# Recurrent and latent stages in one block, w_out begun with its own splits, group means as two rounded products

## The reference, cut to what matters

```python
def group_layer_norm(x, g, b, n_groups):          # first block, convolution branch, 8 groups of 128
    mu = jnp.mean(xf, axis=-1, keepdims=True)
    var = jnp.mean(jnp.square(xf - mu), axis=-1, keepdims=True)
    y = ((xf - mu) * lax.rsqrt(var + EPS)).reshape(shp)
...
    o = rms_norm(o, onorm_g.reshape(HG_HEADS, HG_HEAD_DIM))   # first block, each head of 128
...
    y = jnp.concatenate([y_conv, y_hgrn.astype(y_conv.dtype)], axis=-1)
    h = h + y @ w_out[i].astype(y.dtype)
    pe = p[i] @ w_pp[i].astype(p.dtype)
    gate = jax.nn.sigmoid(rms_norm(h, pe_norm_g[i]) @ w_pg[i].astype(h.dtype))
    h = h + gate * pe.astype(h.dtype)
...
        u = rms_norm_2(h, norm_mix_g[l])                      # second block
        proj = u @ w_in[l]
        x_rnn, g_rnn, q_c, kv_c, k_pe, gate_logits = jnp.split(proj, split_points, axis=-1)
        xa = causal_conv(x_rnn, conv_w[l], conv_b[l])
        ya = rg_lru(xa, ...) * jax.nn.gelu(g_rnn)             # recurrent stage
        yb = mla(q_c, kv_c, k_pe, positions, ...)             # latent stage, attention
```

## Time and profile before

| | |
|---|---|
| median of 3 runs | 2914.78 us (2914.42 to 2917.72) |
| profiled execution, own time | 2912.4 us |
| its span | 2910.4 us |
| mean granted TensorE clock | 0.971 of full speed |
| PE busy | 2719.5 us (93%) |
| DVE busy | 1652.7 us (57%) |
| ACT busy | 1234.8 us (42%) |
| loop over heads, first start of `scores(i, 0)` to the last | 136.8 to 752.9 us |
| w_out's first product | 934.98 us |
| first latent product | 1676.16 us |

### The profile page before, as it was taken

One profiled execution on the slowest core, in us unless ns is written; L12 is line 12 of the kernel. 1 busy time (PEld: TensorE's weight loads), 2 busy tenths in 40 slices (PEclk: granted clock), 3 DMA queues, 4 the chain that ended last, 5 costly groups with the idle time before them and its releaser, 6 DMA issues. The chain is left out here.

```text
span 2910.4 us, 33765 instructions
## 1 busy us (share of the span) xinstructions
PE 2719.5 (93%) x12640; PEld 2148.8 (74%) x12640; DVE 1652.7 (57%) x2524; ACT 1234.8 (42%) x1733; POOL 206.3 (7%) x183
## 2 busy tenths in 40 slices
PE   7999999999998999999999998999999989599993
PEld 5888888888876887768777697777767668477772
DVE  5788888888532314434324233666767663666664
ACT  4244443434421214634433424555555542266661
POOL 0010111110100000000000000000000000442213
PEclk9999999999999999999999998999999999699997
DMA  5333232332335120112112020000000131899997
GB/s 183 109 120 123 87 102 94 105 105 98 127 119 188 48 102 22 44 58 70 46 50 65 29 80 21 24 15 24 15 24 16 58 75 45 342 358 341 356 363 269
DMA packets 168688, 329.06 MB, mean 113 GB/s; under 512 B 17831, under 2 KB 125480, under 8 KB 154840
## 3 DMA queue, kind: packets, MB, share of 16 engines
q1 hardware_dynamic: 152952, 289.25, 28.5%
q0 software_dynamic: 14720, 34.64, 3.2%
q10 hardware_dynamic: 864, 3.15, 0.3%
HBM read 293.94 MB, written 100.16 MB: 135 GB/s over the span
## 5 line engine op out<-in xcount | busy, mean ns | idle before, releaser
L398 PE MATMUL PS<-UHI,WHI 128*128 128x512 f32 x1008 | 416.0, 413 | 4.1 <-DVE ULO L127 4.1
L398 PE MATMUL PS<-ULO,WHI 128*128 128x512 f32 x1008 | 400.3, 397 | 0.0
L398 PE MATMUL PS<-UHI,WLO 128*128 128x512 f32 x1008 | 400.2, 397 | 0.0
L127 DVE TENSOR_TENSOR WLO<-arena,WHI 128x1024 fp32r<-128x1024 f32 x94 | 115.3, 1226 | 213.9 <-ACT WHI L123 213.8
L398 PEld LDWEIGHTS PS<-UHI,WHI 128*128 128x128 f32 x1008 | 190.6, 189 | 52.3 <-issue 5.5
L398 PEld LDWEIGHTS PS<-ULO,WHI 128*128 128x128 f32 x1008 | 190.7, 189 | 47.6 <-issue 5.5
L398 PEld LDWEIGHTS PS<-UHI,WLO 128*128 128x128 f32 x1008 | 190.3, 189 | 46.4
L1238 PE MATMUL PS<-U2HI,WHI 128*128 128x512 f32 x480 | 193.0, 402 | 2.7 <-DVE WLO L127 2.7
L1238 PE MATMUL PS<-U2HI,WLO 128*128 128x512 f32 x480 | 189.5, 395 | 0.0
L1238 PE MATMUL PS<-U2LO,WHI 128*128 128x512 f32 x480 | 189.4, 395 | 0.0
L1888 PE MATMUL PS<-arena 96*128 96x512 f32 (+3 forms) x384 | 155.1, 515 | 12.5 <-ACTq L2030 10.3
(11 more groups left out here) (458 smaller groups left out, 5895.8 us busy)
## 6 DMA issues: line engine op xcount, KB each, us to landing
arena<-in_w_in SPq DMA_DIRECT2D x88, 512.0 KB, 4.0
xd_dram<-in_x SPq DMA_DIRECT2D x32, 768.0 KB, 6.8
y_dram<-in_x SPq DMA_DIRECT2D x32, 768.0 KB, 6.7
arena<-in_w_gate SPq DMA_DIRECT2D x13, 1024.0 KB, 7.2
arena<-in_w_up SPq DMA_DIRECT2D x13, 1024.0 KB, 11.4
arena<-in_w_down SPq DMA_DIRECT2D x13, 1024.0 KB, 14.0
arena<-in_w_out SPq DMA_DIRECT2D x32, 256.0 KB, 2.6
RB<-in_w_gate SPq DMA_DIRECT2D x7, 1024.0 KB, 7.3
```

Of the source, the lines that this page charges most:

```text
L127: return eng.tensor_tensor(dst, src, hi.bitcast(F32), ALU.subtract)
L398: last = pe.matmul(o[:, h * HALF:(h + 1) * HALF], x[:, k, :], y[:, k, h * HALF:(h + 1) * HALF], start=(k == r == 0), stop=(k == ND - 1 and ...
```

## The change

**Means.** The mean matrix is rounded once into `MEANR` (1/128 is exact). For each mean ACT now rounds the operand into `AVGHI` and DVE computes the remainder into `SQLO` or `HSQLO`; PE does two rounded products per half (high and remainder) instead of one in plain float32. New on ACT: `conv_hi(i)` behind `head_root(i - 1)`, and a rounding behind the square in `conv_square` and `head_square`. New on DVE: `conv_lo(i)` in front of `update(i, 1)`, `square_lo(i)` behind `masked(i, 3)`, `head_square_lo(i)` in front of the last two taps.

**Order in the loop.** On PE `conv_var` goes from behind `scores(i, 3)` to behind `scores(i, 4)`. On ACT `conv_root` goes from behind `mix(i, 4)` to behind `mix(i, 5)`, and `conv_out` from behind `mix(i, 5)` to behind `mix(i, 6)`. On DVE `norm` goes from behind `update(i, 4)` to behind `update(i, 5)`. Scores 5 and 7 use other banks, with waits to match.

**Blocks.** A `retire` (which keeps five semaphores) now stands between the first block and w_out. The latent block is merged into the block of w_out and the recurrent stage, with no barrier and no `retire` between. SP loads the first four latent chunks before it stores the last gate; ACT and DVE split the first two before the last evacuation of the recurrent stage; the rotary tables move from chunk 1 to chunk 3.

**w_out.** ACT and DVE begin with the splits of chunk 0; the feature copies come behind them (PE waits for these only ahead of its fifth output tile), and the recurrence constants go to chunk 18.

```diff
-        SCORES = [LOW] + [PS[:, b, :] for b in (6, 4, 5, 4, 6, 5, 6)]
+        SCORES = [LOW] + [PS[:, b, :] for b in (6, 4, 5, 4, 5, 4, 5)]
...
-                def mean_of(o, v, done):
+                def mean_of(o, hi, lo, done):
                     for h in range(2):
-                        last = pe.matmul(o[:, h * HALF:(h + 1) * HALF], mean, v[:, h * HALF:(h + 1) * HALF],
-                                         start=True, stop=True)
+                        for r, v in enumerate((hi, lo)):
+                            last = pe.matmul(o[:, h * HALF:(h + 1) * HALF], MEANR[:], v[:, h * HALF:(h + 1) * HALF],
+                                             start=(r == 0), stop=(r == 1))
...
-                    if q in (2, 3, 4):
-                        pe.wait_ge(s_amask, (LEVELS + 1) * i + (1, 1, 3)[q - 2])
-                    elif q == 5:
-                        pe.wait_ge(s_croot, i + 1)
-                    elif q >= 6:
-                        pe.wait_ge(s_amask, (LEVELS + 1) * i + (4, 6)[q - 6])
+                    if q >= 2:
+                        pe.wait_ge(s_amask, (LEVELS + 1) * i + max(1, q - 1))
...
                 def turn_keys(i):
                     pe.wait_ge(s_upd, LEVELS * (i + 1))
-                    pe.wait_ge(s_amask, (LEVELS + 1) * i + 7)
+                    pe.wait_ge(s_amask, (LEVELS + 1) * (i + 1))
...
                 def state_steps(i):
                     pe.wait_ge(s_kdec, i + 1)
-                    pe.wait_ge(s_amask, (LEVELS + 1) * (i + 1))
+                    pe.wait_ge(s_croot, i + 1)
...
                     scores(i, 3)
-                    conv_var(i)
                     first_half(n + 2)
                     scores(i, 4)
+                    conv_var(i)
                     second_half(n + 2)
...
+                def conv_hi(c):
+                    act.wait_ge(s_conv, c + 1)
+                    if c:
+                        act.wait_ge(s_oms, c)
+                    split_hi(act, AVGHI[:], ACC[c % 2]).then_inc(s_acchi, 1)
...
                     if i:
                         head_root(i - 1)
+                    conv_hi(i)
                     upper(n + 2)
...
                     mix(i, 4)
-                    conv_root(i)
                     upper(n + 4)
                     mix(i, 5)
-                    conv_out(i)
+                    conv_root(i)
                     evacuate(n + 2)
                     upper(n + 5)
                     mix(i, 6)
+                    conv_out(i)
...
                     taps(c, 3, 5)
+                    conv_lo(i)
                     update(i, 1)
...
                     masked(i, 3)
+                    square_lo(i)
                     taps(c, 8, 11)
                     lower(n + 4)
                     update(i, 4)
-                    norm(i)
                     masked(i, 4)
                     taps(c, 11, 14)
                     lower(n + 5)
                     update(i, 5)
+                    norm(i)
                     masked(i, 5)
...
-                    taps(c, 20, 24)
+                    taps(c, 20, 23)
                     lower(n + 7)
                     state(i)
-                    taps(c, 24, 27)
-                    taps(c, 27, CONV_K)
+                    taps(c, 23, 29)
+                    head_square_lo(i)
+                    taps(c, 29, CONV_K)
...
+        retire(s_held, s_x3, s_ptok, s_wpp, s_yland)
...
-        retire(s_held)
...
+                store_gate(NB - 1, 0)
+                sp.wait_ge(s_mt, 2 * NB)
                 for n in range(NRAW):
-                    load(n)
+                    load_latents(n)
+                store_gate(NB - 1, 1)
+                for t in range(2):
+                    sp.wait_ge(s_sigst[t], 16 * NB)
...
+                    for n in range(4, NX):
+                        if n == NX - 1 and not more:
+                            for k in range(2):
+                                stream_hi(act, k, W6RAW, W6HI, s_w6land, s_w6used, s_w6hi)
+                        evacuate(b, n, more)
...
-                act.wait_ge(s_pturn, 1)
-                act.activation(PFEAT[:, 1, :], banks(6), ACT.Copy).then_inc(s_pfeat, 1)
                 upper(0)
...
                 for n in range(4 * ND):
                     stream_hi(act, n, W3RAW, W3HI, s_w3land, s_w3used, s_w3hi)
+                    if n == 0:
+                        act.wait_ge(s_pturn, 1)
+                        act.activation(PFEAT[:, 1, :], banks(6), ACT.Copy).then_inc(s_pfeat, 1)
+                    if n == 18:
+                        act.wait_ge(s_soft, 1)
+                        act.activation(CREC[1], CREC[1], ACT.Exp, scale=-1.0).then_inc(s_softexp, 1)
```

More of the change, by code:

```diff
@@ new lines, in _ @@
+                sp.wait_ge(s_u2n, NT)
+                for n in range(2, NX):
+                    sp.wait_ge(s_rwlo, n - 1)
+                    load(0, n)
+                    if n == 2:
+                        load_gates(0)
+                with sp.Fori(1, NB) as b:
+                    for n in range(NX):
+                        sp.wait_ge(s_rwlo, NX * b + n - 1)
+                        hold(sp)
+                        load(b, n)
+                        if 1 <= n <= 2:
+                            store_gate(b - 1, n - 1)
+                        if n == 2:
+                            sp.wait_ge(s_ri, 2 * b)
+                            hold(sp)
+                            load_gates(b)
@@ L1816, in _, with project @@
             def _(pe):
+                def project(b, n, halves=(0, 1)):
+                    if halves[0] == 0:
+                        pe.wait_ge(s_rwlo, NX * b + n + 1)
+                        if n >= 2 or not isinstance(b, int):
+                            pe.wait_ge(s_revac, NX * b + n - 1)
+                    o, w = banks(2 * (n % 2)), weight_of(b, n)
+                    for h in halves:
+                        for k in range(ND):
+                            for i, (x, y) in enumerate(passes((w[1][n % 2], w[2][n % 2]), (U2HI, U2LO))):
+                                last = pe.matmul(o[:, h * HALF:(h + 1) * HALF], x[:, k, :],
+                                                 y[:, k, h * HALF:(h + 1) * HALF],
+                                                 start=(k == i == 0), stop=(k == ND - 1 and i == 2))
+                    if h:
+                        last.then_inc(s_rproj, 1)
@@ new lines, in lru_gates @@
+                def lru_gates(b, t):
+                    pe.wait_ge(s_ax, 32 * b + 32)
+                    pe.wait_ge(s_xa, 2 * b + 2)
+                    if t or not isinstance(b, int):
+                        pe.wait_ge(s_riev, 2 * b + t)
+                    for i in range(2):
+                        for h in range(2):
+                            for k in range(2):
+                                last = pe.matmul(banks(4 + 2 * i)[:, h * HALF:(h + 1) * HALF],
+                                                 WAX[:, i, k, t * P:(t + 1) * P],
+                                                 XA[k][:, h * HALF:(h + 1) * HALF], start=(k == 0), stop=(k == 1))
+                    last.then_inc(s_ri, 1)
@@ new lines, in embed @@
+                def embed(m):
+                    if m:
+                        pe.wait_ge(s_gated, m)
+                    else:
+                        pe.wait_ge(s_wpp, 32)
+                        pe.wait_ge(s_h, NT + 6)
+                    for h in range(2):
+                        for k in range(2):
+                            last = pe.matmul(PS[:, 4 + h, :], PFEAT[:, k, m * P:(m + 1) * P],
+                                             WPP[:, k, h * HALF:(h + 1) * HALF], start=(k == 0), stop=(k == 1))
+                    last.then_inc(s_peprod, 1)
@@ new lines, in gate @@
+                def gate(m, k0, k1):
+                    if k0 == 0:
+                        pe.wait_ge(s_nlo, m + 1)
+                        if m < 2:
+                            pe.wait_ge(s_h, NT + 4 + 4 * m)
+                        else:
+                            pe.wait_ge(s_gsig, m - 1)
+                    for k in range(k0, k1):
+                        if m == 0:
+                            pe.wait_ge(s_pglo, k + 1)
+                        for h in range(2):
+                            for i, (x, y) in enumerate(passes((NHI, NLO), (WPGHI, WPGLO))):
+                                last = pe.matmul(PS[:, gate_banks(m) + h, :], x[:, k, m * P:(m + 1) * P],
+                                                 y[:, k, h * HALF:(h + 1) * HALF],
+                                                 start=(k == i == 0), stop=(k == ND - 1 and i == 2))
+                    if k1 == ND:
+                        last.then_inc(s_gprod, 1)
@@ new lines, in _ @@
+                turn_h(0)
+                embed(0)
+                for m in range(NT):
+                    gate(m, 0, 4)
+                    if m:
+                        embed(m)
+                    if m + 1 < NT:
+                        turn_h(m + 1)
+                    gate(m, 4, ND)
```

(11 more changed lines are left out.)

881 lines of the change are left out of this document (406 added, 475 removed).

## The result

The changed kernel takes 2922.4 us (median of 7 runs, 2919.24 to 2929.05) against 2915.56 (7 runs, 2914.42 to 2917.72) before, a ratio of 1.0026 with a 95% interval of 1.0014 to 1.0037. The forecast was 2916.3. The range holds the time; the difference, 6.8 us, lies just above the 0.2% (5.8 us) that the prediction called no change, with the interval on both sides of it. The profiled execution has a span of 2920.3, 9.9 more than before.

| stretch | forecast | measured |
|---|---|---|
| up to the first scores 0 | 0 | +1.1 |
| head 0 | +1.2 | +3.1 |
| heads 1 to 6 | +18.6 | +17.9 |
| head 7 to the last product of the block | -1.5 | +0.3 |
| seam to w_out, and w_out | -6.5 | -4.6 |

A forecast was written before the change was run, and what follows sets the result against it. PE, busy 93% of the span, bounds the kernel, with DVE close behind in the loop. First block +18.3, w_out -6.5, latents -10.3 sum to +1.5: 2913.9 profiled, 2916.3 median. Range 2888 to 2929 us.

The forecast's parts named there:

- The mean: On PE in the loop: a mean costs 0.94 us, 0.77 less than before, for each of 24 means.
- Step 1: Start of a head: conv_hi (1.0 us) and conv_lo (1.2) lie exposed, so DVE's first update starts 6.6 behind scores 0.
- Step 2: PE waits 0.6 us for masked copy 0 before scores 2, and 0.4 for masked copy 1 before the mean.
- step 5: Late in a head: masked copy 7 ends at 56.1 us; PE waits 2.2 before scores 7 and the keys' turn.
- Step 4: Root behind mix 5 delays the weight split and fifth update; PE loses 2.2 us before scores 6.
- Head 7: Last head of the first block: no taps, so no waits, and -1.5 us.
- The seam to w_out: First block to w_out: products start 4.6 us earlier and 1.9 of lost clock returns; -6.5, at the least -4.1.
- The latents: Seam to latents: PE goes straight on, then waits 3.2 us before chunk 4; -10.3 (-13.5 without wait, -8 if clock falls).
- PE never waits in the loop: Rival: DVE's work fits and PE has no loop waits; 2879.5 us, chance 0.12.
- only the root's hole: Rival: only the wait between mix 5 and mix 6 stays, 2.2 us less 2.3 a head; 2895, chance 0.16.
- The clock falls in the new holes: Rival: clock falls in the hole before scores 6, heads 0 to 6, 1.9 us each, 13 together; 2929, chance 0.12.
- The merged block gives nothing back: Rival: at the latents, early loads or splits come no sooner; 2926 us, chance 0.08.

The follow-up runs named there:

- three edits: Changed kernel with the root in front of mix 5, two taps moved forward and the convolution's rounding behind the weight split: 2896.3 us, ratio 0.9935, head 87.6 us.
- four: Changed kernel with root before mix 5, two taps forward, convolution rounding behind the weight split, and scores 7 in bank 6: 2888.3 us, ratio 0.9912, head 86.7 us.
- the taps forward: Changed kernel with two of DVE's convolution taps moved from behind the state recurrence into its wait for a weight split: 2920.0 us, ratio 1.0015.
- the new blocks alone: Changed kernel with the loop of the kernel before; only the merged block, new retire and early w_out stay: 2899.3 us, ratio 0.9949.
- the new means alone: Kernel before with the means of two rounded products and the new loop order, blocks and seams as before: 2936.8 us, ratio 1.0075.
- without remainders: Changed kernel without the means' three remainders on DVE, each mean adding the rounded data twice: 2908.3 us, ratio 0.9980.
- root: Changed kernel with ACT taking the convolution's inverse root before mix 5, not behind it: 2902.3 us, ratio 0.9962.
- later rounding: Changed kernel with ACT rounding the convolution behind the weight split, not in front of it: 2924.0 us, ratio 1.0031.

## Why the prediction was right, and where not

**The mean.** Right: 0.92 for 0.94.

**Step 1, the chain from the head's mean.** Right that `conv_hi` and `conv_lo` come exposed before update 1, wrong in what follows. I had update 1 at 6.6 behind scores 0; it is at 4.66, because scores 0 itself starts later, behind the hole before `pad`'s reader. **Step 2's** waits before scores 2 (0.6) and the mean (0.4) are absent for the same reason.

**The step that failed** is the sentence behind step 5: "`state`, the taps and `head_square_lo` (1.2) have room", resting on DVE's wait of 3.62 in the earlier trace rows. That wait lies behind `pad`; before it there is little room. The rows of before that I had not costed (DVE, and the head's mean on PE):

```profile
372.86 1.23 DVE L127 TENSOR_TENSOR WLO<-arena,WHI 128x1024 fp32r<-128x1024 f32 x1 [2.10 <-ACT WHI L123]
...
387.25 0.69 DVE L820 TENSOR_TENSOR arena<-PS,arena 128x512 f32<-128x512 f32 x1
```

```profile
387.89 1.88 PE L443 MATMUL PS<-RC,square 128*128 128x512 f32 x4
```

`pad`'s first half was there at 387.94, and PE, with a mean of 1.71 from 387.89, wanted it at 389.60: 1.66 of slack. From the split's remainder to the end of that half are 15.08 before and 17.61 after (382.19 to 399.80), 2.53 more: the new remainder and one more tap. The mean is 0.77 shorter. 1.66-2.53-0.77 = -1.64, the hole of 1.63.

**Step 4, the root.** The mechanism was right: DVE's wait of 2.6 measured 2.44, and its removal gave 2.5 a head. PE shows only 1.13 before scores 6, since the hole before `pad`'s reader has made it late already. With 0.16 for each hole, PE has lost 1.8+1.3 = 3.1 up to scores 6; the walk had 1.0+2.2 = 3.2.

**Step 5, scores 7 and the keys' turn.** 2.2 forecast, 0.78+1.05 measured, 2.15 with 0.16 for each; the bank alone is worth 0.95 of it (three edits against four).

**The loss a head** was forecast as 5.4 over PE's own 85.8, and 91.1-85.8 = 5.3 measured. The walked chain closes on itself (head mean, head root, splits, DVE's list, update 5, masked copy 7, the keys' turn, the next head mean), and its length was right: with the taps forward, where 1.06 of `pad`'s hole is gone, a head still takes 91.1. Which stretch of PE pays for it is another matter, and there I was wrong. That the way over `pad`, which I had not costed, came out equal and not longer is luck: both reach update 2 within 0.1 us. Head 0 has the full +3.1 because what I let it save lies in front of its scores 2, and the holes (1.11, 0.78, 1.05, 1.63 there too) lie behind; head 6 has only +1.7, since no `pad` follows it.

**Head 7** has no taps, as said. That a hole of 3.68 stands before the products of the last splits, where it was 2.89, is the last mean, 0.77 shorter, which the forecast had rightly not counted as a gain. But I had "no waits", and scores 6 met a hole of 0.67, behind the root. The rest of the way from -1.5 to +0.3 is clock, about 1 us behind that hole before the last splits' products, in the changed kernel and in the kernel before (windows of PE; 24 products against 28 in 8 us):

```profile
853.31:861.31 8.00, 8.00 (x24) 0.66 0.48 162
```

```profile
831.88:839.88 8.00, 8.00 (x28) 0.79 0.51 159
```

**The seam to w_out.** First product 4.3 earlier for 4.6: `retire` cost 2.73-1.65 = 1.08 for my 1.0, and from the barrier's end to the first product 4.3 passed for my 4.2. The term that failed is the 1.9 of clock, which I had the shorter hole give back; here only 0.3 came of it. With the new blocks alone it did come: 6.6 less for my 6.5. The Trainium skill, "TensorE: Matmul & The Clock Gate", section "What's actually happening", has activity as what releases the clock; the 4.6 that the prediction worked out by that rule is what this profile shows, and not that of the new blocks alone, where a like hole cost no clock.

**The latents.** The mechanism was right, wait and all (3.2 forecast, 2.62 measured): from the gate store to chunk 4's load pass 7.15 us (1688.39 to 1695.54), where I had 8.0. -9.1 for -10.3. With the new blocks alone the clock did not fall there, and the stretch took 10.9 less; here it fell behind the hole before chunk 4 (window of PE), the case for which I had given -8:

```profile
1705.75:1707.75 2.00, 2.00 (x7) 0.50 0.48 130
```

**The recurrent stage** holds a difference that no step had, and no edit made (one window before, one after):

```profile
1261.50:1267.50 6.00, 5.94 (x25) 4.81 (x26) 0.03 (x3) 0.02 (x1) 0.00 (x0) 1.00 0.51 164
```

```profile
1279.30:1285.30 6.00, 5.97 (x14) 4.72 (x15) 0.00 (x0) 0.00 (x0) 0.00 (x0) 0.50 0.53 170
```

These are the same products before and after, behind the same hole of 2.37 us. At half the clock they cost 2.9 us more. The kernel with the new means alone, that with the new blocks alone and that without remainders kept the full clock there; the seven other variants did not, and lost 1.3 to 2.9.

**The time as a whole.** Between the forecast's +1.5 and the +9.9 of the profiled execution lie 8.4 us. About 6 are clock (1.9 at w_out, 2.9 in the recurrent stage, 1.2 at the latents), 3.7 are heads 0 and 7, of which 1 is clock again; the rest takes 1.2 back.

**The rivals.** "PE never waits in the loop" and "only the root's hole" fell with the rows above. "The clock falls in the new holes" did not come true inside the loop of the changed kernel (1.00 from 130 to 780 us, with holes of up to 1.98), and held at the seams, where it was not placed. It was a near thing: two variants lost 1.5 us behind such a hole of the loop once and twice, at `pad`'s reader and not before scores 6. "The merged block gives nothing back" fell: -15.8.

## What to carry to other kernels

A saving on the busiest engine can be worth nothing in a loop whose other engines must deliver on a serial path: here 2.3 us of PE a head came with 5.3 of waits, and four changes of order, with no work removed, turned +21.7 us into about -11 (2888.3 against the 2899.3 of the blocks alone). To find the path, look not at the engine that shows the hole but at what the engines upstream wait for (ACT idle for 7.08 us beside the root that everybody waited for), and read slack at each consumer of its own: a wait further down the same list is no room for what comes before it. When removing a hole gives nothing, look for a second way of the same length to the same consumer, and try both edits together. And look at the granted clock stretch by stretch before a few us are put down to an edit: it fell in places that the edit had not touched.

## What the runs showed of the hardware

Whether TensorE's clock falls behind a hole of 2 to 3.7 us is not settled by its length. Behind the 2.37 us of the recurrent stage the granted clock fell to 0.50 in 8 of 12 profiles (the two kernels and the ten variants) and stayed at 1.00 in 4. In the loop, in heads 3 and 4 of four kernels (changed, means alone, root, later rounding), the hole before `pad`'s reader was 1.97 to 2.01: it fell behind three of these eight. Behind the loop's holes of up to 1.78 it never fell. At w_out, in the ten with the merged block, it fell in 7. In four of them it fell just behind the second hole (2.40 to 2.56 us), and in three it had fallen among the transposes, behind the first (2.73 or 2.74); these then took longer, which left a second hole of only 1.49 to 1.67. It stayed full in 3, with second holes of 2.28, 2.43 and 2.45 behind first ones of 2.71 to 2.74. Behind the 3.68 us at the end of the first block it stayed full in two variants (root, later rounding). At w_out, in the loop and in the recurrent stage a fall cost 1.3 to 2.9 us, as much as several terms of the forecast; what decides it stays open.

Of six taps of DVE beside POOL's products (386.24 to 395.13) four took 1.28 us each, as the taps without POOL do. The second, beside the end of POOL's longest product (2.13 us from 386.29), took 1.91, and the third 1.48; 0.8 us a head, in the kernel before as well:

```profile
387.59 1.91 DVE L853 SCALAR_TENSOR_TENSOR RC<-arena,cols,RC 128x1024 f32<-128x1024 f32 x1
```

The Trainium skill, "GPSIMD Engine Reference", section "1. Specifications", has the SBUF interfaces of the two engines shared, with contention for DVE's instructions with two SBUF inputs; two of the six agree, and four show no price.
